# Three-block transformer kernel on one core: both norms between the layers by token half, and the first chunk of products behind them by token half

## The reference: what is computed

```python
def first_block(...):
    for i in range(2):
        h = rms_norm(x, pre_norm_w[i])
        y = gated_deltanet_mixer(h, ...) if i == 0 else short_conv_mixer(h, ...)
        x = x + rms_norm(y, post_norm_w[i])
    return x

def second_block(x, c, ...):
    shift, scale, gate = jnp.split(c @ w_ada + b_ada, 3, axis=-1)
    h = rmsnorm(x, pre_norm_g) * (1.0 + scale) + shift
    ...                       # retention and convolution branches, merged, w_out
    return x + gate * rmsnorm(y, post_norm_g)
```

## Time and profile before

| | before |
|---|---|
| median of 3 runs | 909.13 us (908.52 to 911.43) |
| profiled execution, its own time | 913.8 us |
| its span, first to last instruction | 911.7 us |
| TensorE busy, weight loads busy | 883.2 us (97%), 821.0 us (90%) |
| DVE busy, ScalarE busy | 698.0 us (77%), 510.0 us (56%) |
| mean granted clock | 0.982 |
| a 1 MB weight chunk of `gdn_out`, issue to landing (median) | 5.3 us |

### The profile page before, as it was taken

One profiled execution on the slowest core, in us unless ns is written; L12 is line 12 of the kernel. 1 busy time (PEld: TensorE's weight loads), 2 busy tenths in 40 slices (PEclk: granted clock), 3 DMA queues, 4 the chain that ended last, 5 costly groups with the idle time before them and its releaser, 6 DMA issues.

```text
span 911.7 us, 16439 instructions
## 1 busy us (share of the span) xinstructions
PE 883.2 (97%) x6456; PEld 821.0 (90%) x6456; DVE 698.0 (77%) x1116; ACT 510.0 (56%) x729; POOL 46.5 (5%) x48
## 2 busy tenths in 40 slices
PE   5999999989989999999999999999999999999997
PEld 5999998779867999999998889999887799999995
DVE  5777889835665777777767677899999999956774
ACT  6598877535454655555545555333345675435642
POOL 0001110122010000000000000000001130001000
PEclk9999999959999999999999989999999999999999
DMA  8735564610367467777778516555555445555441
GB/s 254 234 111 184 177 201 140 172 56 1 112 208 235 139 221 249 243 254 250 246 243 307 191 47 226 167 185 186 166 171 171 139 139 185 185 192 176 137 143 47
DMA packets 139474, 161.57 MB, mean 177 GB/s; under 512 B 17155, under 2 KB 112283, under 8 KB 139419
## 3 DMA queue, kind: packets, MB, share of 16 engines
q1 hardware_dynamic: 139419, 160.80, 54.4%
HBM read 156.58 MB, written 4.21 MB: 176 GB/s over the span
## 4 chain that ended last, share of the span: by engine, by line
PE 77%; DVE 16%; ACT 5%; issue 2%; DMA 1%; SPq 0%; DVEq 0%; ACTq 0%
PE psum L480 23%; PE psum L481 23%; PE psum L482 23%; DVE w_lo L1383 5%; DVE cv L1826 3%; PE psum L770 3%; DVE Tq L1611 1%; DVE outer L1609 1%; ACT w_hi L939 1%; DVE cacc L1532 1%; PE psum L640 1%; PE psum L752 1%; PE psum L876 1%; PE psum L652 1%; DMA x<-in_x_dram 1%
## 5 line engine op out<-in xcount | busy, mean ns | idle before, releaser
L1383 DVE TENSOR_TENSOR w_lo<-w_raw,w_hi 128x1024 fp32r<-128x1024 f32 x264 | 316.7, 1222 | 121.2 <-ACT w_hi L939 119.9
L939 ACT ACTIVATE w_hi<-w_raw 128x1024 fp32r<-128x1024 f32 x264 | 274.9, 1057 | 210.3 <-PE psum L482 169.0
L480 PE MATMUL psum<-hT_hi,w_hi 128*128 128x256 f32 x1216 | 348.3, 286 | 4.4 <-DVE w_lo L1383 3.5
L481 PE MATMUL psum<-hT_lo,w_hi 128*128 128x256 f32 x1216 | 345.8, 284 | 0.0
L482 PE MATMUL psum<-hT_hi,w_lo 128*128 128x256 f32 x1216 | 345.7, 284 | 0.0
L480 PEld LDWEIGHTS psum<-hT_hi,w_hi 128*128 128x128 f32 x1216 | 235.1, 193 | 6.0 <-issue 4.9
L481 PEld LDWEIGHTS psum<-hT_lo,w_hi 128*128 128x128 f32 x1216 | 235.1, 193 | 0.3 <-issue 0.2
L482 PEld LDWEIGHTS psum<-hT_hi,w_lo 128*128 128x128 f32 x1216 | 235.2, 193 | 0.0
L1826 DVE SCALAR_TENSOR_TENSOR cv<-aP,par,cv 128x256 f32<-128x256 f32 x240 | 106.7, 511 | 0.0
L480 PE MATMUL psum<-w_hi,hT_hi 128*128 128x512 f32 x224 | 91.3, 408 | 1.7 <-DVE w_lo L1383 1.7
L482 PE MATMUL psum<-w_hi,hT_lo 128*128 128x512 f32 x224 | 87.4, 390 | 0.0
(11 more groups left out here) (287 smaller groups left out, 1076.1 us busy)
## 6 DMA issues: line engine op xcount, KB each, us to landing
w_raw<-in_w_in_dram SPq DMA_DIRECT2D x44, 1024.0 KB, 5.0
w_raw<-in_sc_w_in_dram SPq DMA_DIRECT2D x32, 1024.0 KB, 7.4
w_raw<-in_gdn_w_in_dram SPq DMA_DIRECT2D x24, 1024.0 KB, 6.2
ada<-in_w_ada_dram SPq DMA_DIRECT2D x24, 512.0 KB, 5.0
w_raw<-in_gdn_w_out_dram SPq DMA_DIRECT2D x8, 1024.0 KB, 5.3
w_raw<-in_sc_w_out_dram SPq DMA_DIRECT2D x8, 1024.0 KB, 8.8
w_raw<-in_w_ret_out_dram SPq DMA_DIRECT2D x8, 1024.0 KB, 5.2
w_raw<-in_w_conv_out_dram SPq DMA_DIRECT2D x4, 1024.0 KB, 5.1
```

Of the source, the lines that this page charges most:

```text
L480: pe.matmul(o, l_hi, r_hi, start=start, stop=False, skip_group_check=True)
L481: pe.matmul(o, l_hi, r_lo, start=False, stop=False, skip_group_check=True)
L939: act.activation(w_hi[j % 2 * 2 + h][:, :, :], raw[slot][:, h * KH2:(h + 1) * KH2, :], ACT.Copy).then_inc(hi_ready, 1)
L1383: return dve.tensor_tensor(o, whole, hi.bitcast(F32), ALU.subtract)
```

## The change

It has three parts.

First, at both norms the conversion of h goes by token half too. ScalarE's `h_high` and DVE's `h_low` make 128-token pieces of `hT_hi` and `hT_lo` for the first half before the second half has been normed. Second, chunk 0 of `sc_in` and of `glu` is done by `chunk_by_token`: all 48 products for the first 128 tokens, then filling matmuls or the rest of the modulation and the transposes of the second half, then the 48 products for the other 128 tokens. The filling goes from 4, 3, 1 to 4, 1, 2 matmuls at the first norm and from 3 to 1 at the second. Third, in the rounds `turn_y` moves: on TensorE to ahead of the half chunk of its round, on ScalarE to the head of the round, and that of the last group into round 17. `junk`, a buffer for squares that nobody reads, moves by 8 KB.

```diff
+            def turn_x(n, t):
+                for k in range(KT):
+                    if k % KH2 == 0:
+                        pe.wait_ge(xn_ready, (NT * n + t) * 2 + k // KH2 + 1)
+                    mm = pe.transpose(bank(4 + k // 2, P)[:, k % 2 * NT + t, :], xn[:, t, k * P:(k + 1) * P], ident)
+                    if k % 2 and (n or t == NT - 1):
+                        mm.then_inc(turned, 1)
+
+            def chunk_by_token(n, g0, between):
+                pe.wait_ge(bank_free, g0 + 1)
+                for t in range(NT):
+                    rows = slice(t * P, (t + 1) * P)
+                    for h in range(2):
+                        if t == 0:
+                            pe.wait_ge(lo_ready, 2 * g0 + h + 1)
+                        for m in range(2):
+                            mine = slice(m * P, (m + 1) * P)
+                            for k in range(KH2):
+                                ka = h * KH2 + k
+                                if m == 0 and k % 2 == 0:
+                                    pe.wait_ge(h_ready, norm_pair(n, t, ka // 2))
+                                mm = product(bank(0)[:, m, rows], w_hi[h][:, k, mine], w_lo[h][:, k, mine], hT_hi[:, ka, rows], hT_lo[:, ka, rows],
+                                             t == 0 and m == 0 and ka == 0, ka == KT - 1)
+                        if t:
+                            mm.then_inc(half_done, 1)
+                    if t == 0:
+                        between()
+                        turn_x(n, 1)
...
                 if 3 <= r < 11:
                     level6_s(r - 3)
+                for p in range(NPAIR):
+                    if r == STAGE1[p] + 7:
+                        turn_y(p)
                 if r >= OUT_FROM:
                     c, h = (r - OUT_FROM) // 2, (r - OUT_FROM) % 2
                     wide_half(FIRST["gdn_out"] + c, h, 0, yT_hi, yT_lo, c * KH2, c == 0, False, (y_op_ready, 0))
-                for p in range(NPAIR - 1):
-                    if r == STAGE1[p] + 7:
-                        turn_y(p)
-            turn_y(NPAIR - 1)
...
-            pre_norm(1, (4, 3))
+            keep_clock(4)
+            turn_x(1, 0)
             keep_clock(1)
-            phase("sc_in", hT_hi, hT_lo, True, operand=(h_ready, KT // 2))
+            phase("sc_in", hT_hi, hT_lo, True, operand=(h_ready, norm_pair(1, 0, 0) - 1), normed=(1, lambda: keep_clock(2)))
...
             modulation(0, range(2 * KT))
-            pre_norm(2, (0, 3))
-            modulation(2, range(2 * KT, 3 * KT))
+            turn_x(2, 0)
+            keep_clock(1)
...
+            phase("glu", hT_hi, hT_lo, True, operand=(h_ready, norm_pair(2, 0, 0) - 1), beside=gate_rows,
+                  normed=(2, lambda: modulation(2, range(2 * KT, 3 * KT))))
```

On ScalarE and DVE:

```diff
+            def h_high(n, t):
+                rows = slice(t * P, (t + 1) * P)
+                for kp in range(KT // 2):
+                    if n == 1:
+                        act.wait_ge(turned, norm_pair(n, t, kp))
+                        for k in range(2):
+                            i = act.activation(hT_hi[:, 2 * kp + k, rows], bank(4 + kp)[:, k, rows], ACT.Copy,
+                                               scale=gain1[:, KT + 2 * kp + k:KT + 2 * kp + k + 1])
+                    else:
+                        act.wait_ge(hx_ready, t * (KT // 2) + kp + 1)
+                        i = act.activation(hT_hi[:, 2 * kp:2 * kp + 2, rows], hx[:, 2 * kp:2 * kp + 2, rows], ACT.Copy)
                     i.then_inc(hhi_ready, 1)
...
                         y_root(1)
                         if n < 2:
+                            h_high(n + 1, 0)
                             x_squares(n + 1, 1)
+                            split_hi(FIRST[ORDER[ORDER.index(name) + 1]], 0, 1, 0)
+                            h_high(n + 1, 1)
...
             for r in range(ROUNDS):
                 for p in range(NPAIR):
+                    if r == STAGE1[p] + 7:
+                        turn_y(p)
+                for p in range(NPAIR):
                     if 1 <= r - STAGE1[p] + 1 <= 6:
                         apply(p, r - STAGE1[p] + 1)
...
                         y_piece(n, b, 1, 1)
-                        if n < 2:
-                            normed(n + 1, 0)
-                        x_next(n, 1)
+                        if n == 2:
+                            x_next(n, 1)
+                            return
+                        normed(n + 1, 0)
                         if between is not None:
                             between()
-                        if n < 2:
-                            normed(n + 1, 1)
+                        h_low(n + 1, 0, (0, 1))
+                        x_next(n, 1)
+                        h_low(n + 1, 0, (2, 3))
+                        normed(n + 1, 1)
+                        h_low(n + 1, 1, (0, 1))
+                        h_low(n + 1, 1, (2, 3))
+                        split_lo(FIRST[ORDER[ORDER.index(name) + 1]], 0, 1, 0)
```

More of the change, by code:

```diff
@@ L67, with norm_pair @@
 CHUNKS = _g
+def norm_pair(n, t, kp):
+    return KT // 2 + ((n - 1) * NT + t) * (KT // 2) + kp + 1 if n else kp + 1
 ADA = 3
@@ L566, in wide_deep, with keep_clock, phase @@
                         wide_half(g0 + c, h, c // 4 * 2, a_hi, a_lo, c % 4 * KH2, c % 4 == 0, c % 4 == 3, operand if c < 4 else None)
-            def phase(name, a_hi, a_lo, channels, deep=False, operand=None, beside=None, loop_beside=None):
+            def keep_clock(times):
+                for _ in range(times):
+                    pe.matmul(bank(1, P)[:, 0:C_LOW + 1, :], ident, const[:, 0:C_LOW + 1, :], start=True, stop=True)
+            def turn_x(n, t):
[25 more added lines that the diff above has]
+                        turn_x(n, 1)
+            def phase(name, a_hi, a_lo, channels, deep=False, operand=None, beside=None, loop_beside=None, normed=None):
                 g0 = FIRST[name]
@@ L578, in step @@
                     for j in range(4):
-                        if deep:
+                        if normed is not None and isinstance(i, int) and 4 * i + j == 0:
+                            chunk_by_token(normed[0], g0, normed[1])
+                        elif deep:
                             chunk(i, g0, j, j // 2, a_hi, a_lo, j % 2 * KT, channels, j % 2, operand if j == 1 else None)
@@ L595, in phase @@
                         step(i + (n - KT // 4), i)
+                elif normed is not None:
+                    step(0)
+                    with pe.Fori(1, COUNT[name] // 4) as i:
+                        step(i)
                 else:
                     loop(pe, COUNT[name] // 4, step)
[L599 to L611, removed]
             pe.wait_ge(ident_loaded, 16)
@@ new lines, in low_of_pair, with first_norm @@
+            def low_of_pair(kp, gain, rows):
+                for k in (2 * kp, 2 * kp + 1):
+                    i = dve.scalar_tensor_tensor(out=hT_lo[:, k, rows], in0=bank(4 + kp)[:, k % 2, rows], scalar=gain[:, k:k + 1],
+                                                 in1=hT_hi[:, k, rows].bitcast(F32), op0=ALU.mult, op1=ALU.subtract)
+                i.then_inc(h_ready, 1)
+            def first_norm(gain, between):
+                for t in range(NT):
+                    normed(0, t)
+                between()
+                for kp in range(KT // 2):
+                    dve.wait_ge(hhi_ready, norm_pair(0, 0, kp))
+                    low_of_pair(kp, gain, slice(0, SEQ))
+                    if kp == KT // 4 - 1:
+                        split_lo(0, 0, 0, 0)
@@ new lines, in h_low @@
+            def h_low(n, t, pairs):
+                rows = slice(t * P, (t + 1) * P)
+                if n == 2:
+                    for kp in pairs:
+                        dve.wait_ge(turned, norm_pair(n, t, kp))
+                        for k in (2 * kp, 2 * kp + 1):
+                            i = dve.tensor_scalar(hx[:, k, rows], bank(4 + kp)[:, k % 2, rows], gain2[:, k:k + 1], mod[:, k:k + 1], ALU.mult, ALU.add)
+                        i.then_inc(hx_ready, 1)
+                for kp in pairs:
+                    dve.wait_ge(hhi_ready, norm_pair(n, t, kp))
+                    if n == 1:
+                        low_of_pair(kp, gain1[:, KT:2 * KT], rows)
+                    else:
+                        pair = slice(2 * kp, 2 * kp + 2)
+                        part_lo(hT_lo[:, pair, rows], hx[:, pair, rows], hT_hi[:, pair, rows]).then_inc(h_ready, 1)
```

76 lines of the change are left out of this document (18 added, 58 removed).

## The result

The changed kernel takes 926.25 us, the median of 6 runs (924.12 to 931.64), beside 909.74 us for the kernel before on the same chip (908.52 to 911.43). The ratio is 1.019, 95% interval 1.0156 to 1.0224, so 14 to 20 us slower. The profiled execution took 931.64 us, the longest of the six; its span is 929.6 us for 911.7, its mean granted clock 0.967 for 0.982. As the clock has two levels, a mean of c over a span s is worked out as 2 x (1 - c) x s at 1.2 GHz: 61 us in the profiled execution, 37 to 50 us in the other five, and 33 us in the profiled execution of the kernel before.

What follows compares the result with a forecast made beforehand. TensorE, busy for 97% of the span, was taken to bound the kernel. Rounds -2.5, first norm +3.8 and second norm +14.5 sum to 15.8 us, put on the 909.13 median: 925 us, range 912 to 937 (8 in 10).

Steps and rivals of the forecast that it cites:

- A narrow product's price: In the half chunks: a 128-column product taken at 0.11 us, so chunk 0 costs 10.6 us for 5.8.
- The rivals' 0.066 and 0.236: Rival prices in us of a 128-column product: load hidden and columns deciding, or paid like plain fp32 (chance 0.19).
- not slower: Rival, chance 0.11: in the half chunks the load hides, a product costs 0.066 us; sum -0.6 us, 908.5.
- First norm, +3.8: At the first norm: second half chunk ends at 308.5 against 304.73, 3.8 us later.
- Second norm, +14.5 at the low clock: At the second norm: half chunks, modulation and transposes at 1.2 GHz, second half chunk ending 14.5 us later.
- up to 3 us more: Behind the second norm: possible extra loss of up to 3 us where chunk 1 starts at 1.2 GHz.
- I expect the low clock to stay until chunk 1: At the second norm: 1.2 GHz lasts through both half chunks, a product taking 0.215 us.
- 1 to 3 less: At the second norm: 1 to 3 us less loss if the clock is up for part of the first half.
- The rounds, -2.5: At the end of the delta-rule rounds: holes go, V of round 13 is 2.8 late, chunk 3 starts 2.5 us earlier.
- 5.3 us: At the end of the rounds: upper bound of the gain, if ScalarE's order costs nothing.
- Full clock, same price: Rival, chance 0.2: half chunks keep 2.4 GHz or regain it in the first; sum +5 us, 914.

Runs made afterwards that it cites:

- e3_norm1: Kernel before, with only the first norm's conversion and chunk 0 by token half; rounds and second norm as before: 915.50 us, ratio 1.0052.
- e4_norm2: Kernel before, with only the second norm's conversion and chunk 0 by token half; rounds and first norm as before: 924.08 us, ratio 1.0157.
- the run with both clock edits: Changed kernel, second norm with 3 filling matmuls for 1, modulation's last third behind chunk 0 of glu, 2 filling matmuls in its place: 918.91 us, ratio 1.0077.
- e7_price: Kernel before, with one chunk of sc_in as 48 products of 192 columns and 48 of 64 instead of 48 of 256: ratio 1.0081.
- e1_rounds: Kernel before, with only the rounds part of the change (turn_y moved on TensorE and ScalarE), both norms as before: 909.79 us, ratio 0.9978.
- e11_fill3: Changed kernel, with 3 filling matmuls instead of 1 ahead of the second norm's first half chunk: 925.22 us, ratio 1.0166.
- e12_modlate: Changed kernel, with the modulation's last third behind chunk 0 of glu and 2 filling matmuls in its place: 924.30 us, ratio 1.0138.
- e8_narrow: Kernel before, with two chunks of sc_in as 192 products of 128 columns instead of 96 of 256: 922.24 us, ratio 1.0115.

## Why the prediction was right, point by point

The forecast was 925 us, slower; measured were 926.25. The sum of +15.8 us became +17.3 (14 to 20). The price of a product, the first norm and the rounds came out as worked out; that the second norm's term fits the mean as well as the profile is in part luck, as said below.

- **A narrow product's price is the weight load.** 0.11 forecast; 0.112 at 1.00 and 0.2135 to 0.22 at 0.50 measured, and at 1.00 the same for 64 and 192 columns. The rivals' 0.066 and 0.236 are out, which was decisive against "not slower". That it is the load and not another fixed price of a product stays an inference. The 81 ns for 128 columns of the Trainium skill (TensorE: Matmul & The Clock Gate, Back-to-back issue gap) is not reached by these products of rounded float32: the measured 0.112 decides.
- **First norm, +3.8.** The trace has +3.86, and the part alone measured +4.7 (3.1 to 6.4). The steps are right too: xn of the second half was ready 2.2 us before its transposes; one wait of 0.71 for `hT_lo`, products at full clock. That full clock was not sure: e3_norm1's execution lost it there and paid about 5 us more, an outcome that the text did not price.
- **Second norm, +14.5 at the low clock.** +15.25 in the trace, +14.3 (11.5 to 17.1) measured alone. The clock fell within the one-column matmuls, a little earlier than the text had it (they took 4.50 us for 3.63, which is the 0.75 that 15.25 has over 14.5), and stayed low to chunk 1 and 3.0 us into it, which the text had as "up to 3 us more". The step that was too simple is "I expect the low clock to stay until chunk 1": it did in the profiled execution, the slowest of the six, but in the trace of the same code in e4_norm2 the first half chunk ran at 2.4 GHz for the most part, and three of the changed kernel's six executions had at least 6 us less of the low clock at this norm than the profiled one. So 14.5 is one of at least two outcomes of one program, and the text priced only the one (its "1 to 3 less" was too little for the other: e4_norm2 took 6.8 us less to chunk 1).
- **The rounds, -2.5.** -2.51 in the trace, -2.0 (-3.7 to -0.3) measured. V of round 13 was to end 2.8 us late and chunks 2 and 3 to start at 253.15 and 260.2; less 0.69 this is 252.46 and 259.51, and they stand at 252.41 and 259.52. That 5.3 us were to be had if ScalarE's order cost nothing was too high: 3.5 in the trace, since the split ahead of chunk 2 again comes 1.9 us late; the 4.3 of the timed runs go with a higher mean clock as well.
- **"Full clock, same price"** (914) is what the run with both clock edits comes near to: +7.0 for a rival's +5. It was the right mechanism for a kernel with the filling and the place of the modulation that this one lacks.
- The sum was put on the median though made against a profiled execution; the profiled one came out at 931.6, +17.8 over its predecessor. Here luck helped. Both profiled executions were slow ones of their kernel, 913.8 over a median of 909.7 and 931.6 over 926.25, so the difference of two slow executions came near to that of the medians.

## What to carry to other kernels

Before a product is split by its moving dimension, read how far apart products of few columns stand in a trace (here 0.11 us): where the columns take no longer than that, half of them cost the same, and splitting nearly doubles the bill whatever it overlaps. Then check what the halves would hide if they were free; here it was nothing, because each half waits for a chain of its own. Judge the order around a wait by the granted clock too: moving the one-column matmuls from ahead of the second half chunk and putting more full-width filling ahead of the first gave back 10 of 17 us. And before a low level in one profile is priced, look at the mean clock of the other executions, since one profile shows one outcome.

## What the runs showed of the hardware that was not expected

- The clock is not fixed by the code. With the same instructions the first norm and chunk 1 behind it ran at 1.00 in the changed kernel and had 10.3 us at 1.2 GHz in e3_norm1; the second norm had from none (e7_price) to 10.3 us of it (e1_rounds) in the old order.
- Five half chunks of 128 columns ran at 1.2 GHz from end to end (10.2 to 10.5 us, 48 products each: two in the changed kernel, one each in e4_norm2, e11_fill3 and e12_modlate) and did not bring 2.4 GHz back. It was back 2.8 to 5.0 us into chunk 1 with its 256 columns (four profiles), and 3.0 us after two filling matmuls began between the half chunks of e12_modlate. At 2.4 GHz products of 128 columns ran for 21 us without losing it in e8_narrow, but not in e3_norm1.
- A dense stream of 64 columns was followed by 6.9 us at the low clock in the one profile there is, with TensorE never idle and the loads 0.11 us apart.
- At 1.2 GHz narrow products are 0.2135 us apart, 1.9 times 0.112, so what sets their price pays the low clock nearly in full.
